# Shifting x, y and weight tiles against each other modulo 512 bytes in a hybrid encoder kernel

## What is computed

```python
h = rmsnorm(x, a_norm); proj = h @ a_w_in            # 2048 -> 2 x 2560
xb, gate = proj[..., :D_RNN], proj[..., D_RNN:]
xb = causal_depthwise_conv(xb, a_conv_w, a_conv_b)   # width 4
y = rg_lru(xb, a_w_r, a_b_r, a_w_i, a_b_i, a_lambda) # two block-diagonal products, then a scan
x = x + (y * silu(gate)) @ a_w_out                   # 2560 -> 2048
kv = rmsnorm(x, kv_norm) @ w_kv                      # 2048 -> k, v of 16 heads x 128
h = rmsnorm(x, b_norm); proj = h @ b_w_in            # 2048 -> q, gate
o = stick_breaking_attention(q, k, v)                # strictly causal, 16 heads
x = x + (o * silu(gate)) @ b_w_out
return rmsnorm(x, final_norm)
```

## Time and profile before

| | |
|---|---|
| median of 2 runs | 1705.97 us (1705.64 to 1706.29) |
| profiled execution | 1707.84 us |
| its span, first to last instruction | 1706.1 us |
| mean granted TensorE clock | 0.998 |
| PE busy | 1691.7 us (99%), 8607 matmuls |
| DVE busy | 909.6 us (53%) |
| ACT busy | 798.0 us (47%) |
| POOL busy | 228.2 us (13%) |
| DMA | 162.22 MB, mean 95 GB/s |

### The profile page before, as it was taken

One profiled execution on the slowest core, in us unless ns is written; L12 is line 12 of the kernel. 1 busy time (PEld: TensorE's weight loads), 2 busy tenths in 40 slices (PEclk: granted clock), 3 DMA queues, 4 the chain that ended last, 5 costly groups with the idle time before them and its releaser, 6 DMA issues.

```text
span 1706.1 us, 25540 instructions
## 1 busy us (share of the span) xinstructions
PE 1691.7 (99%) x8607; PEld 1448.8 (85%) x8607; DVE 909.6 (53%) x1688; ACT 798.0 (47%) x1622; POOL 228.2 (13%) x219
## 2 busy tenths in 40 slices
PE   8999999999999999999999999999999999999998
PEld 7888888888888888888889898988989898898888
DVE  5667676666675344354546455554645455453323
ACT  7655566666555233244445444453444444432223
POOL 0121221212212011021101010111101011112100
PEclk9999999999999999999999999999999999999999
DMA  5333333333333223223232322223232232323223
GB/s 182 99 105 94 98 97 93 91 98 97 100 99 99 94 97 98 92 89 98 75 98 79 90 83 86 86 80 92 81 92 80 86 92 75 98 74 112 93 94 135
DMA packets 155910, 162.22 MB, mean 95 GB/s; under 512 B 9608, under 2 KB 147032, under 8 KB 155736
## 3 DMA queue, kind: packets, MB, share of 16 engines
q1 hardware_dynamic: 155864, 161.63, 30.8%
HBM read 157.39 MB, written 4.19 MB: 95 GB/s over the span
## 4 chain that ended last, share of the span: by engine, by line
PE 98%; ACT 1%; DVE 0%; DMA 0%; issue 0%; POOL 0%; SPq 0%; POOLq 0%; DVEq 0%; ACTq 0%
PE ps L359 96%; PE ps L480 1%; PE ps L388 0%; PE ps L535 0%; DMA xraw<-in_x 0%; DVE rbuf L980 0%; POOL y_lo L1172 0%; ACT w_hi L593 0%; PE ps L395 0%; ACT abuf L677 0%; DVE w_lo L838 0%; DVE tbuf L976 0%; ACT L677 0%; ACT rbuf L665 0%; ACT tbuf L674 0%
## 5 line engine op out<-in xcount | busy, mean ns | idle before, releaser
L359 PE MATMUL ps<-x_hi,w_hi 128*128 128x512 f32 x1408 | 551.7, 392 | 0.0
L359 PE MATMUL ps<-x_hi,w_lo 128*128 128x512 f32 x1408 | 548.8, 390 | 0.0
L359 PE MATMUL ps<-x_lo,w_hi 128*128 128x512 f32 x1408 | 548.7, 390 | 0.0
L841 DVE SCALAR_TENSOR_TENSOR w_lo<-stage,cT,w_hi 128x256 fp32r<-128x256 f32 x416 | 230.5, 554 | 502.2 <-ACT w_hi L597 501.5
L595 ACT ACTIVATE w_hi<-stage,cT 128x256 fp32r<-128x256 f32 x416 | 211.1, 507 | 485.1 <-PE ps L359 484.9
L359 PEld LDWEIGHTS ps<-x_hi,w_lo 128*128 128x128 f32 x1408 | 264.7, 188 | 55.2
L359 PEld LDWEIGHTS ps<-x_hi,w_hi 128*128 128x128 f32 x1408 | 264.9, 188 | 54.5 <-issue 0.7
L359 PEld LDWEIGHTS ps<-x_lo,w_hi 128*128 128x128 f32 x1408 | 265.0, 188 | 54.4 <-issue 0.5
L838 DVE TENSOR_TENSOR w_lo<-stage,w_hi 128x512 fp32r<-128x512 f32 x160 | 129.0, 808 | 244.7 <-ACT w_hi L593 244.7
L593 ACT ACTIVATE w_hi<-stage 128x512 fp32r<-128x512 f32 x160 | 100.6, 631 | 266.8 <-PE ps L359 265.5
L843 DVE SCALAR_TENSOR_TENSOR w_lo<-stage,cT,w_hi 128x256 fp32r<-128x256 f32 x416 | 213.1, 512 | 0.0
(11 more groups left out here) (161 smaller groups left out, 1994.4 us busy)
## 6 DMA issues: line engine op xcount, KB each, us to landing
stage<-in_a_w_in SPq DMA_DIRECT2D x160, 256.0 KB, 2.7
stage<-in_b_w_in SPq DMA_DIRECT2D x128, 256.0 KB, 2.6
stage<-in_w_kv SPq DMA_DIRECT2D x128, 256.0 KB, 2.6
stage<-in_a_w_out SPq DMA_DIRECT2D x80, 256.0 KB, 2.5
stage<-in_b_w_out SPq DMA_DIRECT2D x64, 256.0 KB, 3.1
out<-x SPq DMA_DIRECT2D x8, 512.0 KB, 3.2
xraw<-in_x SPq DMA_DIRECT2D x3, 1024.0 KB, 10.5
stage<-in_a_w_r SPq DMA_DIRECT2D x10, 256.0 KB, 2.9
```

Source lines behind the costliest of these rows:

```text
L359: mm = pe.matmul(dst, a, b, start=start and n == 0, stop=stop and n == 2, skip_group_check=not check)
L841: nc.vector.scalar_tensor_tensor(w_lo[:, slot, 0:256], stage[:, slot, 0:256], cT[:, col:col + 1], f(w_hi[:, slot, 0:256]), ALU.mult, ALU.s ...
```

## The change

A constant SKEW = 8 (numbers, 32 bytes) is added. The tiles of x and y are allocated with rows of 520 numbers instead of 512, and the slots of w_hi and w_lo with 516; views of the first 512 numbers take the place of the tiles, so that all code behind works on them as before.

```diff
@@ -80,6 +80,7 @@
 LINE_GAP = 192
+SKEW = 8
@@ -110,15 +111,15 @@
         stage = sb("stage", [P, RING, 512])
-        w_hi = sb("w_hi", [P, RING, 512], F32R)
-        w_lo = sb("w_lo", [P, RING, 512], F32R)
-        x_hi = sb("x_hi", [P, KD, S], F32R)
-        x_lo = sb("x_lo", [P, KD, S], F32R)
+        w_hi = sb("w_hi", [P, RING, 512 + SKEW // 2], F32R)[:, :, 0:512]
+        w_lo = sb("w_lo", [P, RING, 512 + SKEW // 2], F32R)[:, :, 0:512]
+        x_hi = sb("x_hi", [P, KD, S + SKEW], F32R)[:, :, 0:S]
+        x_lo = sb("x_lo", [P, KD, S + SKEW], F32R)[:, :, 0:S]
 
 
         with ExitStack() as mem12:
-            y_hi = sb("y_hi", [P, KR, S], F32R, mem12)
-            y_lo = sb("y_lo", [P, KR, S], F32R, mem12)
+            y_hi = sb("y_hi", [P, KR, S + SKEW], F32R, mem12)[:, :, 0:S]
+            y_lo = sb("y_lo", [P, KR, S + SKEW], F32R, mem12)[:, :, 0:S]
```

## The result

The changed kernel takes 1734.57 us (median of 2 runs, 1734.29 to 1734.84) against 1705.97 us, a ratio of 1.0168 with a 95% interval of 1.0124 to 1.0211. It is slower by 28.6 us, well clear of the spread of the runs. The profiled span grew from 1706.1 to 1733.1 us.

The account below looks back on a forecast made before the run. TensorE, busy 99% of the span, was taken to bound the kernel. Span 1706.1 us plus 0 on TensorE and 0 elsewhere gave 1706 against the median, written as 1707 us for occasional broken settling; range 1655 to 1745 us.

Parts of the forecast that it names:

- rival B: Settling of TensorE's matmuls is broken: +15 us if each half unit starts unsettled, +30 us if none settles; chance 0.22.
- within 2%: Measured time between 1672 and 1740 us, about what a measurement can't tell from no change; chance 0.67.
- The likeliest case, no change: The constant 13.3 ns per TensorE matmul stays, 0 ns change, 1703 to 1712 us; chance 0.42.
- What bounds the kernel, and that only the matmul's cost can move the end: TensorE, busy 99% of the span, bounds it; only shorter or longer matmuls, 226.7 ns at 512 columns, move the end much.
- The other engines, 0: Less aligned splits cost VectorE 0 and ScalarE at most 14 ns each, covered by its waits for TensorE; value 0.
- The constant is the same for pairs in quite different places.: On TensorE, y with w, xc with w and x with w all show 389 to 392 ns, arguing against address dependence.
- The sliding argument: TensorE's two reads slide 535 bytes against each other per weight load, so each load meets any clash once; 0 ns.
- That is the most that the change could gain: Upper bound on TensorE: 7920 matmuls times the constant 13.3 ns, 105 us or 6.2% of the time.
- Rival A: The constant is a clash of TensorE's reads that the skew takes apart: 53 us gained, 1654 us; chance 0.20.
- Rival C: Real slowdown from reads straddling lines or clashing mid-load, 8 ns on all 6000 matmuls, 1754 us; chance 0.14.
- Rival D: Weight splits come late for TensorE, which needs them 400 ns longer; 230 us at twice that growth; chance 0.02.
- Unchanged rows for xc or k: If matmuls slow down, rows with xc or k stay as before, since their tiles are not skewed.

Follow-up runs that it names:

- e6: Only x and y tiles moved, all by the same 128 bytes without skew, against the kernel before; 1736.44 us, ratio 1.0171.
- e11: As e8, but the first twelve matmuls of each 256-column stretch lie 32 bytes further instead of 64; 1699.1 us, ratio 0.9952 against the kernel before.
- e2: Only x and y tiles skewed as in the change, weight slots as in the kernel before; 1732.03 us, ratio 1.0143 against that kernel.
- e3: Only weight slots skewed as in the change, x, y and all behind at 0, against the kernel before; 1733.7 us, ratio 1.0158.
- e5: Separate benchmark of 165 matmul series at combinations of operand places, computing nothing of the kernel; 256-column mean 118.0 ns against 120.0 at equal places.
- e8: Against the kernel before, only units with weights in 256-column pieces lie 64 bytes further in their slot; 1703.39 us, ratio 0.9977.

## Why the prediction was right or wrong

The range (1655 to 1745 us) and the size of rival B held; so did "within 2%", by the ratio of 1.0168, though not by the whole of its interval. The likeliest case, no change, did not: by the prediction's own sign it is wrong once the mean of a 512-column matmul in the long pieces leaves 225 to 229 ns, and that mean is 231.8. That the time still fell inside the range is owed to its width, which came from the rivals and not from the value of 0 ns that the argument gave. By its own steps:

- *What bounds the kernel, and that only the matmul's cost can move the end.* Held. 24.6 of 27.0 us are in three kinds of pieces of the chain, and ScalarE's waits for TensorE grew with it, by 34 us.
- *The other engines, 0.* Held: splits 508 instead of 507 ns, no wait that is new.
- *"The constant is the same for pairs in quite different places."* This was the step that failed: it put the price of a distance at 0 ns, and the kernel paid 5.1 ns on each of the 2052 matmuls of the first long piece. All those pairs were at the same place modulo 256 bytes. Rows 6 had no pair at another distance, as the text itself says, so they were no evidence about distance at all.
- *The sliding argument* (each load meets each distance once, so the skew only moves the clash). It fell. With a fixed distance of 128 bytes the price is 6.7 ns in the series and 5.6 ns in e6. Its hidden assumption was that a clash costs the same wherever it falls within a load; that this is where it went wrong is argued here, since no run looks inside a load. At 512 columns no arrangement tried was cheaper than the one before.
- *"That is the most that the change could gain", 105 us.* The bound was far too wide. Of 92 series at 512 columns none was below 226.7 ns, so on the 6000 matmuls none of the places tried had anything to give, and on the 1920 of 256 columns at most 6.7 ns, 13 us. Rival A had 0.20 for a gain that was not there; the best layout found, e11, is 8.5 us below the kernel before.
- *Rival B, "no matmul ever settles, 5 ns x 6000 = 30 us, 1736 us".* The time is right to 2 us, and that is partly luck. The price came from the scores' matmuls behind the 256-column stretch at 396 and 397 ns, at equal places but outside the settled state, and happens to be near that of a lasting distance. Its mechanism was only half right: settling is real (after a change back to equal places series need up to ten matmuls to return to 226.7), but a fixed distance does not settle to 226.7 either (e6). Its first half, 15 us for a change every six matmuls, was short of the 25 us of e2 alone, since six matmuls behind a change cost some 23 ns and not 15. How much of the changed kernel's loss is owed to lasting distances and how much to changes between them, no run divides.
- *Rival C, "a clash now in the midst of each load", 48 us.* Nearest in kind: a price on each matmul that lasts as long as the places do. It was put at the worst excess, 8 ns; the mean measured is 5.1 ns, and the lowest and highest of the scan are 2.2 and 13.3 ns over equal places. Whether the cause is a clash of two reads is not shown.
- *Rival D, late splits.* Did not occur: no wait of TensorE for w_lo is in the changed profile.
- *"Unchanged rows for xc or k."* Right for k, whose mean stayed at 394 and 393 ns. Wrong for xc: 389 to 394 ns. Its tiles are not skewed, but they start at 384 now and the weights that they meet are skewed, and it is the distance that counts. The same row is 392 ns in e2, where xc starts at 384 and the weights at 0, and 394 in e3, where xc is at 0 and the weights are skewed.
- *256 columns.* Not foreseen: 283 instead of 284 ns on w_hi with x_hi, some 2 us given back in all. In e5 the mean of all distances is 2 ns below equal places at this length.

The Trainium skill ("SBUF — State Buffer", section "Who interferes with whom") gives TensorE two independent read ports, one for each operand. The prediction's step from there to a skew without effect does not hold here: a matmul's time depends on where its moving operand lies relative to its weights (e6, 5 ns in the same program). Whether the two reads meet in a port or elsewhere, no run shows. The Trainium skill ("TensorE: Matmul & The Clock Gate", section "Wait — 56ns, not 53.3ns?") has N / 2.4 GHz plus about 2.5 ns for back-to-back matmuls; the trace agrees for bfloat16 with 215.8 ns at 512 columns and not for these float32r operands, 226.7 ns at best.

What stays open: whether it is the weights in use or the next ones, loaded meanwhile, whose place counts, since no run was made to tell them apart; what makes "both +16" dearer; why equal places are the best at 512 columns and among the worst at 256; what the rest of 13.3 ns at 512 columns is, since no arrangement tried removed it; and what carries the state from one matmul to the next.

## What to carry to other kernels

When a kernel's matmuls already stand at a uniform distance, compare that distance with a short series of the same shape before moving addresses: one kernel of some hundred series answers what the trace of one layout can't. For float32r matmuls of 512 columns, let weights and moving operand start at the same place modulo 256 bytes, hi and lo parts too, and let that place be a multiple of 32 bytes (both at 16 took 230.0 ns); a pad of 64 bytes in front of w_lo cost 1.3% of this kernel and one of 128 in front of x and y 1.7%. A trace in which all operands share one place holds no evidence on whether the place matters.

## What the runs showed that was not expected

- The place of an operand counts modulo 256 bytes and, at the multiples of 32 bytes that were tried, only relative to the other: +128 bytes on everything 1.0001, +256 bytes per slot 0.9998, +128 bytes on x and y alone 1.0171.
- Two lasting states at the same addresses: 256 columns at a distance of 64 bytes run at 113.3 or 117.8 ns a matmul, over 36 matmuls in the series and 84 in the kernel, depending on what came before. In the kernel, steering into the better one for six of eight units brought 4 us beyond e8.
- Skewed halves do not add up: x alone 1.0143, weights alone 1.0158, both 1.0168.
- bfloat16 at 512 columns: 215.8 ns, and no dependence on the distance of 64 bytes.
